# A hybrid decoder layer: stride-16 attention units multiply q with their own 128 key columns instead of 256

## The chip, the cores and the metric

The kernel runs on one core of one Trainium2 chip, as one launch. The metric is the time of an execution on the device in microseconds (us). TensorE (PE) multiplies into PSUM, VectorE (DVE) and ScalarE (ACT) read PSUM and work in SBUF, GpSimd (POOL) and SyncE (SP) issue most of the transfers. All data are 4 bytes wide: plain float32, or float32r, a rounded float32 which PE takes as a type of its own.

## The reference

One layer of a decoder with four parallel branches (pooling, dilated attention, short convolution, sliding-window attention) over a prompt of 2048 rows, and one decode step for 8 samples. What matters here is the dilated attention of the prompt: 6 heads of 64, each attended three times, at strides 1, 4 and 16, and mixed by the softmax of the three log-denominators. A stride d folds the 2048 rows into d residues of 2048/d rows; in each, row i reads the rows i-128 to i.

```python
DIL_CONFIGS = ((128, 1), (512, 4), (2048, 16))
def _fold(a, d):
    n, l, h, dh = a.shape
    return a.reshape(n, l // d, d, h, dh).transpose(0, 2, 1, 3, 4).reshape(n * d, l // d, h, dh)
def _dilated_prompt(q, k, v, slopes):
    for window, d in DIL_CONFIGS:
        o, lse = _band_attention(_fold(q, d)[:, :, :, None], _fold(k, d), _fold(v, d), slopes[:, None], d)
...
    return _mix_dilations(outs, lses)
```

In `_band_attention`, for each block of 128 rows with the 128 rows before it:

```python
    s = jnp.einsum("nbqhgd,nbkhd->nbhgqk", qb, kw, preferred_element_type=jnp.float32) * (1.0 / math.sqrt(dh))
    s = jnp.where(valid[None, :, None, None], s + bias, -jnp.inf)
    p = jnp.exp(s - m[..., None])
    o = jnp.einsum("nbhgqk,nbkhd->nbqhgd", p.astype(v.dtype), vw, preferred_element_type=jnp.float32)
```

At stride 16 a residue has exactly 128 rows, so it is one block with no block before it: its 128 queries need 128 keys, masked to the causal half.

## The kernel before, in words

The program has three parts. First the input projection: 30 tiles of 128 output columns, each product of a high and a low half in three matmuls (lines 929 to 931). Then the attention of the prompt, in three rounds, of which each takes two dilated heads; between these, the decode step's pieces. Then the output projection, row block by row block, with the same lines 929 to 931.

A round is a list of units; a unit is one block of 128 queries for two heads. Rounds one and two have 64 units: 16 at stride 1, 16 at stride 4, 16 at stride 16, and 16 of the sliding window (also stride 1). Round three has 48 and takes them in the order stride 16, 4, 1. The class `Unit` (line 455) gives for a unit its residue `r`, its block `b`, and the slices of q, keys and values. q, and the keys as a high and a low half (`kh_st`, `kl_st`), lie in SBUF as 128 partitions by 2048 rows in float32r, so that a residue at stride 16 is every 16th column: 128 columns, 64 bytes apart.

On PE the body of a round (`attend`, line 1109) runs in steps; step s issues the scores of unit s (line 1022), the transposes of unit s-3's probabilities (line 1038, matmuls at line 1045), the value product of unit s-5 (line 1048, matmuls at line 1061), and every fourth step the transposes of four outputs (line 1070). The scores are two matmuls a head, q times the high and q times the low half of the keys (lines 1034 and 1035), q being the operand that is loaded as weights and the keys the one that streams. They go to one of two PSUM banks, 256 columns a head; before a bank is used again PE waits for VectorE's pass over it (`x_ready`).

VectorE adds the bias and takes the minimum (line 1694), ScalarE takes the exponential (line 1302), PE transposes the probabilities, VectorE copies them out of PSUM (lines 1680 and 1682), PE multiplies them with the values. A unit that has a block before it (`full`) takes all 256 columns through this, any other 128: `own` says at which column these begin, `cols` and `halves` use it.

At stride 16 no unit is full. Its scores nevertheless stream 256 keys: `keys` returns the columns of two neighbouring residues, and `own` is 0 for the even one of them and 128 for the odd one, so that VectorE, ScalarE and the transposes take the right half, and the other half of PSUM is left unread.

VectorE also works on the decode step inside the rounds (lines 1578 to 1592 in rounds one and two, `decode` in round three). The loads of the next pair's q, keys and values are issued by SyncE when the last stride-16 unit's values are done (lines 725 to 727), since they overwrite the tiles that the units read.

Of the kernel before, what the change touches and what calls it, by code (L numbers as in the profile page):

```python
# [19 lines left out]
P = 128  # L20
# [55 lines left out]
def build_program(nc, x_prompt, x_sample, c_t, w_ada, b_ada, norm_g, w_tiles, const, pool_w, pool_scale,  # L76
# [4 lines left out]
    with ExitStack() as ctx:  # L81
# [4 lines left out]
        class Plan:  # L86

            def __init__(self, at):
                self.at = at
# [161 lines left out]
        psum = ctx.enter_context(nc.psum_tensor("psum", [P, 8, 512], F32))  # L251
# [203 lines left out]
        class Unit:  # L455

            def __init__(self, kind, c, i):
                self.kind, self.c, self.i = kind, c, i
                d = 1 if kind else DILATIONS[c]
                self.r, self.b = (0, i) if d == 1 else (i // 4, i % 4) if d == 4 else (i, 0)  # L460
                self.d = d
                self.full = self.b > 0

                self.own = P if self.full or (d == 16 and self.r % 2) else 0

            def view(self, t):
                return t[:].rearrange("p (t r) -> p r t", r=self.d)
# [4 lines left out]
            def keys(self, stack, h):  # L472
                v = self.view(stack[self.kind][h])
                if self.d == 16:
                    r0 = self.r - self.r % 2
                    return v[:, r0:r0 + 2, :]
                c0 = P * (self.b - 1) if self.full else 0
                return v[:, self.r, c0:c0 + 256]

# [30 lines left out]
        S_BANK, PT_BANK, OT_BANK, ON_BANK, DEC_BANK = 0, 2, 4, 6, 7  # L510
# [371 lines left out]
        def _(pe):  # L882
# [139 lines left out]
            def scores(base, n, u, i):  # L1022
                if u.kind and u.i == 0:
                    pe.wait_ge(swa_loaded, 16 * SWA_DMAS * (i + 1))
                if n == 0 and u.c:
                    for j in range(4):
                        pe.wait_ge(piece_loaded[j], 16 * PIECE_DMAS * (i + 1))
                if not u.kind and u.c == 0 and u.i % 4 == 0:
                    pe.wait_ge(piece_loaded[u.i // 4], 16 * PIECE_DMAS * (i + 1))
                if n >= 2:  # L1030
                    pe.wait_ge(x_ready, base + n - 1)
                for h in range(2):
                    out = psum[:, S_BANK + n % 2, 256 * h:256 * h + 256]
                    pe.matmul(out, u.q(h), u.keys(kh_st, h), start=True, stop=False)  # L1034
                    m = pe.matmul(out, u.q(h), u.keys(kl_st, h), start=False, stop=True)  # L1035
                m.then_inc(s_done, 1)
# [72 lines left out]
            def attend(i, us):  # L1109
                base, gbase, n = 64 * i, 16 * i, len(us)  # L1110
                for s in range(n + OUT_LAG + 1 - 4):
                    if len(us) < len(units):
                        decode(s)
                    if s < n:
                        scores(base, s, us[s], i)
                    if TURN_LAG <= s < n + TURN_LAG:
                        turn_probs(base, s - TURN_LAG, us[s - TURN_LAG])
                    if PV_LAG <= s < n + PV_LAG:
                        weigh_values(i, base, gbase, s - PV_LAG, us[s - PV_LAG])
                    if s >= OUT_LAG and (s - OUT_LAG) % 4 == 0:  # L1120
                        turn_out(gbase, (s - OUT_LAG) // 4)
# [825 lines left out]
```

## Time and profile before

| | us |
|---|---|
| median of 3 runs | 1496.07 (1495.25 to 1500.08) |
| span of the profiled execution, first to last instruction | 1494.0 |
| PE busy | 1370.9 (92%) |
| VectorE busy | 715.1 (48%) |
| ScalarE busy | 462.9 (31%) |
| score matmuls, lines 1034 and 1035, 352 each | 148.9 and 123.9 |
| transposes of probabilities, line 1045 | 96.8 |
| value products, line 1061 | 102.5 |

The page lists no time of the profiled execution beside its span; the runs' median lies 2.07 us above that span. Busy times of PE overlap one another, since a matmul's record runs to its last write, so the distance between starts tells more than a duration. PEld are the weight loads, which run beside the matmul before. The attention lies between 828 and 1233 us of the span: round one to 964, round two from 971 to 1103, round three from 1114. The granted clock is given in parts of 2.4 GHz; it has two levels, 1.2 and 2.4 GHz, so that 0.50 in a stretch means that all of it ran at 1.2.

### The profile page before, as it was taken

What the parts mean: (1) busy time and instruction counts of PE and PEld (TensorE: products, weight loads), DVE (VectorE), ACT (ScalarE), POOL (GpSimd) and SP (SyncE); (2) the same over time, 40 slices, a digit from 0 to 9 for tenths busy, and PEclk for the clock granted to TensorE, in tenths of its full rate; (3) what the DMA queues carried; (4) which work ended last, traced back from release to release, by engine and by line L of the source; (5) the groups of instructions that cost most, each with busy time, mean ns of one, the idle gap of its engine ahead of it and who ended that gap; (6) DMA issues with size and microseconds to landing.
All of it is one profiled execution on the core that took longest, in us unless ns stands there. A gap on an engine that the chain in (4) does not pass through costs nothing.

```text
span 1494.0 us, 21742 instructions
## 1 busy us (share of the span) xinstructions
PE 1370.9 (92%) x7749; PEld 1189.5 (80%) x7749; DVE 715.1 (48%) x1835; ACT 462.9 (31%) x1190; POOL 155.0 (10%) x170
## 2 busy tenths in 40 slices
PE   5779999999999999999996799799969997999996
PEld 2376999999999998999996687588757765877774
DVE  3491111100344544132112557676767646788784
ACT  5530000121111001121111455565647641433331
POOL 0060000000122110000000012101110000111111
PEclk9989999999999999999998799999989998999998
DMA  8613121221353434446435992972394255555531
GB/s 311 220 55 121 57 84 42 84 84 43 113 198 121 149 114 141 128 118 167 104 80 127 250 264 85 240 202 63 92 267 132 87 173 177 158 174 155 174 126 45
DMA packets 127167, 206.34 MB, mean 138 GB/s; under 512 B 14339, under 2 KB 89764, under 8 KB 121549
## 3 DMA queue, kind: packets, MB, share of 16 engines
q1 hardware_dynamic: 113862, 160.13, 36.7%
q0 software_dynamic: 13216, 45.09, 9.1%
q8 instruction: 48, 0.79, 0.2%
q14 instruction: 41, 0.34, 0.1%
HBM read 136.34 MB, written 68.97 MB: 137 GB/s over the span
## 4 chain that ended last, share of the span: by engine, by line
PE 68%; issue 14%; DVE 6%; DMA 4%; SPq 4%; ACT 2%; POOL 2%; DVEq 0%; POOLq 0%; ACTq 0%
PE psum L929 15%; PE psum L930 14%; PE psum L931 14%; PE psum L1034 5%; PE psum L1061 5%; PE psum L1045 4%; PE psum L1035 4%; SPq L427 2%; PE psum L900 2%; DMA dil_v_p<-kv_nat 2%; PE psum L1070 1%; POOL resid L876 1%; DVE h_f L1435 1%; DMA v_dil<-dil_v_p 1%; PE psum L1103 1%
## 5 line engine op out<-in xcount | busy, mean ns | idle before, releaser
L929 PE MATMUL psum<-h_hi,w_hi 128*128 128x416 f32 (+1 forms) x1200 | 422.9, 352 | 12.7 <-POOL h_lo L808 12.6
L930 PE MATMUL psum<-h_lo,w_hi 128*128 128x416 f32 (+1 forms) x1200 | 420.8, 351 | 0.0
L931 PE MATMUL psum<-h_hi,w_lo 128*128 128x416 f32 (+1 forms) x1200 | 419.5, 350 | 0.0
L929 PEld LDWEIGHTS psum<-h_hi,w_hi 128*128 128x128 f32 x1200 | 226.7, 189 | 17.7 <-issue 14.9
L930 PEld LDWEIGHTS psum<-h_lo,w_hi 128*128 128x128 f32 x1200 | 226.6, 189 | 1.5
L931 PEld LDWEIGHTS psum<-h_hi,w_lo 128*128 128x128 f32 x1200 | 226.4, 189 | 1.3
L1302 ACT ACTIVATE probs<-logits,stats 128x256 f32<-128x256 f32 (+1 forms) x352 | 162.2, 462 | 172.2 <-DVE stats L1694 169.7
L1034 PE MATMUL psum<-kh_st,q_st 128*128 128x256 f32 x352 | 148.9, 431 | 40.4 <-DMA v_dil<-dil_v_p 30.6
L1694 DVE CUSTOM_DVE_ANT_0 logits<-psum,bias_dil 128x256 f32<-128x256 f32 (+1 forms) x288 | 94.4, 363 | 108.0 <-PE psum L1035 88.5
L1034 PEld LDWEIGHTS psum<-kh_st,q_st 128*128 128x128 f32 x352 | 93.5, 266 | 63.7 <-issue 38.0
L929 PE MATMUL psum<-wo_hi,y_hi 128*128 128x512 f32 x288 | 116.8, 406 | 11.0 <-DVE y_lo L1764 10.6
L1035 PE MATMUL psum<-kl_st,q_st 128*128 128x256 f32 x352 | 123.9, 361 | 0.0
L931 PE MATMUL psum<-wo_hi,y_lo 128*128 128x512 f32 x288 | 113.9, 396 | 0.0
L930 PE MATMUL psum<-wo_lo,y_hi 128*128 128x512 f32 x288 | 113.8, 395 | 0.0
L1515 DVE SCALAR_TENSOR_TENSOR main_lo<-psum,main_hi 128x416 fp32r<-128x416 f32 (+1 forms) x45 | 26.2, 583 | 164.8 <-ACT main_hi L1264 164.8
L1508 DVE COPY main<-psum 128x416 f32<-128x416 f32 (+1 forms) x60 | 34.2, 582 | 143.6 <-PE psum L931 143.6
L1045 PE MATMUL psum<-consts,probs 128*128 128x128 f32 x574 | 96.8, 283 | 3.4 <-DVE probs_t L1682 3.4
L1216 ACT CAST w_hi<-w_raw 128x1024 fp32r<-128x1024 f32 x30 | 31.3, 1043 | 211.3 <-PE psum L931 189.2
L1035 PEld LDWEIGHTS psum<-kl_st,q_st 128*128 128x128 f32 x352 | 96.0, 273 | 0.0
L1680 DVE COPY probs_t<-psum 128x512 f32<-128x512 f32 x111 | 76.7, 691 | 23.5 <-PE psum L1061 22.8
L1061 PE MATMUL psum<-probs_t,v_dil 128*64 128x128 f32 x900 | 82.1, 291 | 0.0
L1045 PEld LDWEIGHTS psum<-consts,probs 128*128 128x128 f32 x574 | 73.0, 146 | 9.3 <-issue 6.8
(244 smaller groups left out, 1560.2 us busy)
## 6 DMA issues: line engine op xcount, KB each, us to landing
w_raw<-w_tiles POOLq DMA_DIRECT2D x30, 512.0 KB, 5.9
mix_dram<-o_st POOLq DMA_DIRECT2D x36, 264.0 KB, 3.6
mix_in<-mix_dram SPq DMA_DIRECT2D x16, 594.0 KB, 4.0
gate_dram<-main SPq DMA_DIRECT2D x9, 1024.0 KB, 3.9
qk_dram<-main_hi SPq DMA_DIRECT2D x18, 512.0 KB, 6.1
qk_dram<-main_lo SPq DMA_DIRECT2D x18, 512.0 KB, 7.8
x_in<-x_prompt SPq DMA_DIRECT2D x16, 512.0 KB, 5.9
ada_w<-w_ada SPq DMA_DIRECT2D x4, 2048.0 KB, 10.0
```

The source lines that it names most:

```text
L929: pe.matmul(out, hi, mhi, start=start, stop=False)
L930: pe.matmul(out, hi, mlo, start=False, stop=False)
L931: return pe.matmul(out, lo, mhi, start=False, stop=stop)
L1034: pe.matmul(out, u.q(h), u.keys(kh_st, h), start=True, stop=False)
L1035: m = pe.matmul(out, u.q(h), u.keys(kl_st, h), start=False, stop=True)
L1045: m = pe.transpose(psum[:, PT_BANK + n % 2, P * k:P * k + P], probs[n % 4][:, h, c:c + P], ident)
L1061: m = pe.matmul(psum[64 * h:64 * h + 64, OT_BANK + g % 2, P * (n % 4):P * (n % 4) + P], u.v(h, back), probs_t[n % 2][:, k, :], start=(x == ...
L1216: nc.scalar.copy(w_hi[b][:], w_raw[b][:]).then_inc(w_hi_ready, 1)
L1302: m = nc.scalar.activation(probs[s % 4][:, h, u.cols()], xs_[s % 2][:, h, u.cols()], ACT.Exp, scale=-1.0, bias=st[:, s % 4, 2 * h:2 * h + ...
L1508: last = dve.tensor_copy(main[b][:, c0:c0 + n], bank(g, n))
L1680: dve.tensor_copy(dst[:], src).then_inc(pt_copied, 1)
L1694: m = dve.tensor_tensor_reduce(out=xs_[s % 2][:, h, c], in0=psum[:, S_BANK + s % 2, 256 * h + c.start:256 * h + c.stop], in1=u.bias(h), sc ...
```

## The change

A unit at stride 16 streams its own residue's 128 keys: `keys` returns one residue, the matmul's output is 128 columns wide instead of 256, and `own` is 0 for odd residues too, so that these use PSUM columns 0 to 127 of their head's 256 like the even ones. Units at strides 1 and 4 and of the window stay as they are. The number and the order of the instructions on every engine are the same before and after; in the listing of PE's instructions 128 rows differ (those of a loop's body and of round three), each by its number of columns, 128 instead of 256. In an execution these are 192 matmuls.

```diff
@@ class Unit
-                self.own = P if self.full or (d == 16 and self.r % 2) else 0
+                self.own = P if self.full else 0
...
             def keys(self, stack, h):
                 v = self.view(stack[self.kind][h])
                 if self.d == 16:
-                    r0 = self.r - self.r % 2
-                    return v[:, r0:r0 + 2, :]
+                    return v[:, self.r, :]
...
@@ scores, on PE
                 for h in range(2):
-                    out = psum[:, S_BANK + n % 2, 256 * h:256 * h + 256]
+                    out = psum[:, S_BANK + n % 2, 256 * h:256 * h + (P if u.d == 16 else 256)]
                     pe.matmul(out, u.q(h), u.keys(kh_st, h), start=True, stop=False)
                     m = pe.matmul(out, u.q(h), u.keys(kl_st, h), start=False, stop=True)
```

## Rows read from the trace of the kernel before

**Rows 1.** Page, head and part 1: engine, busy us (share) xinstructions.

```profile
span 1494.0 us, 21742 instructions
...
PE 1370.9 (92%) x7749; PEld 1189.5 (80%) x7749; DVE 715.1 (48%) x1835; ACT 462.9 (31%) x1190; POOL 155.0 (10%) x170
```

**Rows 2.** Page, part 4: chain of waits by line, share of span.

```profile
PE psum L929 15%; PE psum L930 14%; PE psum L931 14%; PE psum L1034 5%; PE psum L1061 5%; PE psum L1045 4%; PE psum L1035 4%; SPq L427 2%; PE psum L900 2%; DMA dil_v_p<-kv_nat 2%; PE psum L1070 1%; POOL resid L876 1%; DVE h_f L1435 1%; DMA v_dil<-dil_v_p 1%; PE psum L1103 1%
```

**Rows 3.** Stretches: us, busy us (count): PE PEld DVE ACT POOL; clock, DMA, GB/s.

```profile
914.00:926.00 12.00, 12.00 (x72) 9.78 (x72) 7.25 (x28) 6.80 (x28) 4.79 (x8) 1.00 0.45 121
...
1130.00:1140.00 10.00, 10.00 (x60) 8.04 (x60) 7.35 (x31) 8.62 (x29) 0.39 (x1) 1.00 0.24 61
```

**Rows 4.** Timeline, stride-16 unit: start us, us, engine, line, operation.

```profile
913.75 0.29 PEld L1034 LDWEIGHTS psum<-kh_st,q_st 128*128 128x128 f32 x1 [0.17 <-issue]
...
913.96 0.31 PEld L1035 LDWEIGHTS psum<-kl_st,q_st 128*128 128x128 f32 x1
...
914.39 0.31 PEld L1035 LDWEIGHTS psum<-kl_st,q_st 128*128 128x128 f32 x1
...
914.59 0.40 PE L1035 MATMUL psum<-kl_st,q_st 128*128 128x256 f32 x1
...
914.64 0.32 PEld L1045 LDWEIGHTS psum<-consts,probs 128*128 128x128 f32 x2
...
914.80 0.40 PE L1045 MATMUL psum<-consts,probs 128*128 128x128 f32 x2
...
915.50 0.29 PEld L1034 LDWEIGHTS psum<-kh_st,q_st 128*128 128x128 f32 x1 [0.17 <-issue]
```

**Rows 5.** Timeline, PE and PEld, end of a window unit's scores (stride 1).

```profile
944.50 0.19 PEld L1035 LDWEIGHTS psum<-kl_st,q_st 128*128 128x128 f32 x1
944.61 0.29 PE L1035 MATMUL psum<-kl_st,q_st 128*128 128x256 f32 x1
944.63 0.47 PEld L1045 LDWEIGHTS psum<-consts,probs 128*128 128x128 f32 x4
944.74 0.60 PE L1045 MATMUL psum<-consts,probs 128*128 128x128 f32 x4
```

**Rows 6.** Timeline, PEld, first weight load of the third round.

```profile
1114.10 0.29 PEld L1034 LDWEIGHTS psum<-kh_st,q_st 128*128 128x128 f32 x1 [10.90 <-issue]
```

**Rows 7.** Groups by line and shape: busy us, mean ns of one.

```profile
L1034 PE MATMUL psum<-kh_st,q_st 128*128 128x256 f32 x352 | 148.9, 431 | 40.4 <-DMA v_dil<-dil_v_p 30.6 <-issue 7.1 <-DVE stats L1694 2.7
...
L1061 PEld LDWEIGHTS psum<-probs_t,v_dil 128*64 128x64 f32 x900 | 47.1, 137 | 24.8 <-issue 20.8 <-DVE probs_t L1680 3.5 <-DVE probs_t L1682 0.5
```

**Rows 8.** Waits of PE: us in total, times, longest us.

```profile
PE psum L1045 <- DVE probs_t L1682: 3.4, 8, 0.7
PE psum L1034 <- DVE stats L1694: 2.7, 3, 1.9
```

**Rows 9.** Timeline, PE, two neighbouring stride-16 units, third round.

```profile
1123.70 0.56 PE L1034 MATMUL psum<-kh_st,q_st 128*128 128x256 f32 x1
...
1125.88 0.60 PE L1034 MATMUL psum<-kh_st,q_st 128*128 128x256 f32 x1
```

**Rows 10.** Timeline, SP's queue, then PE: the second pair's load.

```profile
936.65 0.32 SPq L420 DMA_DIRECT2D q_st<-qk_dram  x1
...
970.81 0.57 PE L1034 MATMUL psum<-kh_st,q_st 128*128 128x256 f32 x1 [7.12 <-issue]
```

**Rows 11.** Chain in order of time: a decode product on PE.

```profile
1187.31 1.92 PE psum L1103 x6
```

**Rows 12.** Stretches, columns as above: three parts of the program.

```profile
32.00:35.00 3.00, 1.70 (x14) 1.22 (x12) 1.90 (x3) 2.97 (x5) 0.00 (x0) 1.00 0.69 233
...
1070.00:1074.00 4.00, 2.22 (x14) 1.51 (x14) 3.82 (x10) 1.43 (x5) 0.00 (x0) 0.86 0.22 68
1122.00:1126.00 4.00, 4.00 (x20) 3.08 (x18) 2.03 (x14) 2.87 (x14) 0.00 (x0) 0.50 0.81 262
```

## The prediction, made before the changed kernel ran

> **What bounds the kernel now.** Read first the head of the page: TensorE (PE) is busy 1370.9 of 1494.0 us [rows 1]; then the chain of waits, where the projection's three lines hold 43% and the two score lines L1034 and L1035 only 9% [rows 2]. The change touches these two score lines alone, and there only the units at stride 16, so the next view is the table of stretches over the stride-16 units: there PE is busy all the time at the granted clock 1.00, the 2.4 GHz level (12.00 of 12.00 us), VectorE 7.25 and ScalarE 6.80 [rows 3]. PE sets the pace there, so what matters is what paces PE, and that is read from the timeline of one unit.
>
> A stride-16 unit lasts from its first weight load at 913.75 to the next unit's at 915.50, 1.75 us. Its four score matmuls each bring their own load of 128 q columns. The loads start at 913.75, 913.96 and, the fourth, at 914.39: one every 0.215 us. The fourth matmul starts at 914.59, the load for the transposes at 914.64, the first transpose at 914.80 [rows 4]. In a unit of the sliding window, whose q and keys lie side by side, the fourth load starts only 0.11 us before its matmul, and the matmul 0.13 us before the first transpose [rows 5].
>
> Is 0.215 us the price of the load or of the 256 keys? Two things take that long at stride 16. A load alone on an engine that had been idle for 10.90 us takes 0.29 us [rows 6] against 0.19 for the window's [rows 5]. Loads of 64 adjacent columns average 137 ns [rows 7], so 64 columns cost 52 ns more, 128 cost 0.105, and a fixed 0.085 remains; taken from 0.29 to 0.31 us that leaves 0.21 to 0.22 for reading 128 q columns at stride 16. So the load by itself explains the 0.215 us. The fourth matmul is followed by the first transpose after 0.21 us although that transpose's load began 0.16 us before it, where the window needed 0.11: so the 256 strided keys also take about 0.21 us, and hide exactly behind the next load.
>
> The Trainium skill ("TensorE: Matmul & The Clock Gate", section "LDWEIGHTS (loading the stationary operand)") has a load cost its columns over 1.2 GHz, 107 ns for 128, with no word on stride. By that and its "Back-to-back issue gap" section (262 cycles for 256 columns at 2.4 GHz, 134 for 128) load and matmul cost about 108 ns each now and the load stays; the estimated gain would be the last matmul's 53 ns in a unit, 1.5 us over the 29 units counted below. The window's rows agree with the 107 ns, the stride-16 rows are twice that; the conclusion that the load remains is the same.
>
> **The change part by part.** (1) 192 matmuls (3 rounds x 16 units x 2 heads x hi and lo) read 128 keys instead of 256. No instruction is removed, added or moved on any engine, and the 192 weight loads stay as they are. With the loads every 0.215 us, the first three matmuls of a unit gain nothing by being shorter; only the fourth has no strided load behind it. Halved, it ends about 0.105 us earlier, but the transposes' load starts at 914.64 and needs 0.11 us as in the window, so the first transpose moves from 914.80 to 914.75: 0.05 us. If that load also starts 0.02 us after the matmul as in the window, not 0.05, it is 0.08. I take **0.06 us a unit**; the ends are 0 (the load holds the transposes where they are) and 0.105 (the whole half matmul).
>
> (2) Not every unit passes this on. In rounds one and two VectorE has three pieces of decode work among the stride-16 units, and PE then waits for the copied probabilities (8 such waits, 3.4 us, of which the timeline has one a round in the window's units) [rows 8]; each wait swallows the gain of some two units, so 10 of 16 remain. In round three the first seven units wait for a load, for VectorE (up to 1.9 us [rows 8]) and run partly at the low clock; 9 remain. That makes 29 units: 29 x 0.06 = **1.7 us**. Nothing takes it back later: the load of the second pair's keys is issued when the stride-16 values are done (936.65), and PE waits for it until 970.81 [rows 10], so that chain moves as a whole.
>
> (3) Odd units write PSUM and probability columns 0 to 127 instead of 128 to 255. VectorE, ScalarE and the transposes handle the same 128 columns; I cost it at nothing, and their spare time covers a few ns: VectorE is busy 0.60 and ScalarE 0.57 of the first round's stretch, 0.74 and 0.86 of the third's [rows 3].
>
> The sum is -1.7 us on a span of 1494.0; the median of the runs, 1496.07, lies 2.07 above that span, which I carry along: 1496.07 - 1.7 = 1494.4. A measurement of this kernel tells about 0.3% (4.5 us) from no change, so this is no change. The bounds are 0 and 48 x 0.105 = 5.0 us.
>
> **The rivals.** *Keys, not loads, set the 0.215 us (faster).* Were the 0.29 us load only slow in its record, each of the four matmuls would fall to the window's 0.11 us: 0.4 us a unit. Rounds one and two gain 20 x 0.4 = 8; in round three ScalarE's 0.86 of 1.75 us, 1.51, is the next bound, 9 x 0.24 = 2. Together 10, giving 1486. Against it stands the slow load on an idle engine [rows 6]; for it, that matmul and load take the same time, so that no row of a unit separates them.
>
> *Narrow matmuls in this type are dearer per column (no change).* All matmuls on fp32r operands in the trace have 256 columns or more, so the price of 128 is not shown. The nearest row for a dearer one is plain fp32: three decode products of 384 columns take 1.92 us [rows 11], 1.67 ns a column, 0.213 us for 128. That is what 256 strided keys take now, so at the high clock nothing changes; in the six or so units at the low clock, where it would double, up to 0.85 us each is partly covered by the waits of round three. 1496 to 1499, I say 1497.
>
> *The same, with a second weight load (slower).* Plain fp32 matmuls leave two records and two loads each (900 loads for 450 value products, against 352 records for 352 score matmuls [rows 7]). If narrow score matmuls did so too, each would cost another 0.215 us: 48 x 0.86 = 41, less some 5 in waits, 1532. It decides as soon as the count of L1034's records is above 352.
>
> *The clock falls (slower).* With half the keys, PE does less between loads. The granted clock was 0.86 around 1070 to 1074, where PE was busy 2.22 of 4.00 us, and 0.50 at 1122 to 1126 though PE was busy throughout; against that, 1.00 at 32 to 35 with 1.70 of 3.00 us of transposes alone [rows 12]. A stride-16 unit at the 1.2 GHz level takes 1125.88 - 1123.70 = 2.18 us [rows 9] instead of 1.75, so 0.43 more. Over the 29 units that PE paces it is 12.5 less the 1.7: 1507. It decides when more than some 10 of the units run low (4.3 us).
>
> **How the numbers follow.** My forecast has 0.58, dearer narrow matmuls 0.15, keys setting the pace 0.11, a second load 0.06, a falling clock 0.10. The first two are within 0.3%, except for 0.01 of the first at its far end: faster 0.12, same 0.72, slower 0.16. The likeliest time is 1494.4. For 8 in 10 the range takes the first two cases (1491 to 1499) and reaches into the third and the last: 1488 to 1504.
>
> **What would show it.** Right: L1034 and L1035 still have 352 records each, 96 of them with 128 columns; the loads of these still take 0.30 us and one every 0.21 us; the first transpose 0.16 us behind the fourth matmul instead of 0.21; the unit at 1.69 us; clock 1.00 in the stride-16 stretches. Loads closer than 0.2 us prove the first rival, a clock of 0.5 there the last; matmul starts more than 0.22 us apart at the high clock, or more records, mean that a narrow matmul is dear. I am wrong if the unit moves by more than 0.15 us either way.

## The result: slower by 0.7%, and the profile after

The changed kernel takes **1503.84 us** (median of 5 runs, 1503.24 to 1512.19), the kernel before beside it 1495.44 (5 runs, 1493.96 to 1500.08). The ratio is 1.007, with a 95% interval of 1.0045 to 1.0095: the loss is well above the 0.3% below which a measurement of this kernel counts as no change. The profiled execution has a span of 1500.8 us; the span before was 1494.0 [rows 1].

In the changed kernel the lines behind the edit are numbered one lower: the scores are L1033 and L1034, the transposes L1044, the value products L1060. The head of its page, its last line the granted clock of TensorE (PE) in 40 slices of 37.5 us, in tenths of full speed:

```profile
span 1500.8 us, 21742 instructions
...
PE 1378.8 (92%) x7749; PEld 1191.4 (79%) x7749; DVE 716.5 (48%) x1835; ACT 462.7 (31%) x1190; POOL 155.0 (10%) x170
...
PEclk9989999999999999999997998899775997999999
```

The counts are those of before, and PE, which was to work less, is busy 7.9 us longer. The reason stands in the last line: the 25th slice (900 to 938 us) has an 8, the 29th (1051 to 1088) a 7 and the 31st (1126 to 1163) a 5. Each holds part of one round's units at stride 16. In the kernel before all three slices have a 9:

```profile
PEclk9989999999999999999998799999989998999998
```

Cut exactly from the first score record of the first stride-16 unit to the first of the unit behind the sixteenth, the three stretches of the kernel before read as follows (us; busy us and count of PE, weight loads PEld, VectorE, ScalarE, POOL; granted clock, DMA share, GB/s):

```profile
894.59:927.29 32.70, 31.71 (x200) 25.24 (x198) 22.79 (x87) 17.54 (x73) 7.89 (x13) 1.00 0.34 98
1033.15:1065.85 32.70, 31.71 (x200) 25.24 (x199) 22.74 (x87) 17.54 (x73) 7.90 (x13) 1.00 0.29 84
1114.13:1144.72 30.59, 27.93 (x149) 22.13 (x149) 20.98 (x90) 18.63 (x70) 0.75 (x1) 0.84 0.50 141
```

And of the changed kernel, with one more line for six microseconds inside its first stretch and one that answers to [rows 3]:

```profile
890.05:924.58 34.53, 33.50 (x200) 25.89 (x198) 22.98 (x87) 17.46 (x73) 7.90 (x13) 0.80 0.33 96
1030.76:1065.87 35.11, 34.05 (x201) 26.06 (x199) 23.54 (x91) 18.41 (x77) 7.91 (x13) 0.77 0.29 83
1115.20:1150.05 34.85, 32.20 (x148) 23.56 (x148) 22.18 (x92) 18.92 (x71) 0.75 (x1) 0.50 0.42 123
908.00:914.00 6.00, 6.00 (x31) 4.03 (x30) 2.55 (x15) 3.34 (x14) 2.41 (x4) 0.50 0.43 113
...
1130.00:1140.00 10.00, 10.00 (x50) 7.00 (x49) 5.55 (x25) 6.35 (x21) 0.00 (x0) 0.50 0.19 54
```

The rounds lose 1.83, 2.41 and 4.26 us, together 8.5; the medians differ by 8.4. (The profiled span differs by 6.8: in that execution the attention also began 4.15 us earlier, at 824.07 instead of 828.22, and all the rest took 2.5 longer.) The granted clock fell from 1.00 to 0.80 and 0.77 in the first two rounds, and in the third from 0.84 to 0.50, the 1.2 GHz level throughout. In the last two lines PE has no idle time in its records and is still at 1.2 GHz; from 1130 to 1140 it gets through 50 matmul records where it had 60.

A unit of the changed kernel, at either clock. First at 2.4 GHz, its timeline of weight loads and then of PE (start us, us, engine, line, operation):

```profile
918.52 0.30 PEld L1033 LDWEIGHTS psum<-kh_st,q_st 128*128 128x128 f32 x1 [0.17 <-issue]
918.73 0.31 PEld L1034 LDWEIGHTS psum<-kl_st,q_st 128*128 128x128 f32 x1
918.94 0.31 PEld L1033 LDWEIGHTS psum<-kh_st,q_st 128*128 128x128 f32 x1
919.16 0.31 PEld L1034 LDWEIGHTS psum<-kl_st,q_st 128*128 128x128 f32 x1
919.41 0.22 PEld L1044 LDWEIGHTS psum<-consts,probs 128*128 128x128 f32 x2
...
919.25 0.40 PE L1034 MATMUL psum<-kl_st,q_st 128*128 128x128 f32 x1
919.47 0.40 PE L1044 MATMUL psum<-consts,probs 128*128 128x128 f32 x2
919.80 0.44 PE L1060 MATMUL psum<-probs_t,v_dil 128*64 128x128 f32 x4
920.17 0.47 PE L1033 MATMUL psum<-kh_st,q_st 128*128 128x128 f32 x1
```

From 918.52 to 920.17 it takes 1.65 us, 0.10 less than before [rows 4]. The loads still start 0.21 us apart and still take 0.30 us; what came forward is the transposes. Then at 1.2 GHz, PE alone:

```profile
909.70 0.49 PE L1033 MATMUL psum<-kh_st,q_st 128*128 128x128 f32 x1
910.00 0.41 PE L1034 MATMUL psum<-kl_st,q_st 128*128 128x128 f32 x1
910.22 0.41 PE L1033 MATMUL psum<-kh_st,q_st 128*128 128x128 f32 x1
910.44 0.41 PE L1034 MATMUL psum<-kl_st,q_st 128*128 128x128 f32 x1
910.66 0.64 PE L1044 MATMUL psum<-consts,probs 128*128 128x128 f32 x2
911.22 0.70 PE L1060 MATMUL psum<-probs_t,v_dil 128*64 128x128 f32 x4
911.85 0.49 PE L1033 MATMUL psum<-kh_st,q_st 128*128 128x128 f32 x1
```

From 909.70 to 911.85 it is 2.15 us. From the second on, the score matmuls start 0.22 us apart as at the high clock; the half us is lost in the transposes (0.56 us to the next line's start, against 0.33) and the value products (0.63 against 0.37).

### The profile page after: what moved, and what is told of

Its sections match the earlier page's. It is cut to its first block, busy times and chain, and to the rows that moved or that the text cites. A ratio compares the mean times of both kernels' runs of the same rounds, so it can differ in the third digit from the quotient of the medians.

```text
span 1500.8 us, 21742 instructions
## 1 busy us (share of the span) xinstructions
PE 1378.8 (92%) x7749; PEld 1191.4 (79%) x7749; DVE 716.5 (48%) x1835; ACT 462.7 (31%) x1190; POOL 155.0 (10%) x170
## 4 chain that ended last, share of the span: by engine, by line
PE 69%; issue 14%; DVE 5%; SPq 4%; DMA 3%; ACT 2%; POOL 2%; DVEq 0%; POOLq 0%; ACTq 0%
PE psum L928 15%; PE psum L929 15%; PE psum L930 15%; PE psum L1060 5%; PE psum L1033 5%; PE psum L1044 4%; PE psum L1034 4%; SPq L427 2%; PE psum L899 2%; PE psum L1069 2%; POOL resid L875 1%; DVE h_f L1434 1%; DMA v_dil<-dil_v_p 1%; PE psum L1102 1%; DMA ada_w<-w_ada 1%
## 5 line engine op out<-in xcount | busy, mean ns | idle before, releaser
L1033 PE MATMUL psum<-kh_st,q_st 128*128 128x256 f32 (+1 forms) x352 | 143.9, 418 | 44.0 <-DMA v_dil<-dil_v_p 33.7
L1033 PEld LDWEIGHTS psum<-kh_st,q_st 128*128 128x128 f32 x352 | 93.3, 265 | 69.5 <-issue 36.7
L928 PE MATMUL psum<-wo_hi,y_hi 128*128 128x512 f32 x288 | 117.3, 407 | 10.8 <-DVE y_lo L1763 10.5
L1034 PE MATMUL psum<-kl_st,q_st 128*128 128x256 f32 (+1 forms) x352 | 124.2, 361 | 0.0
L1044 PE MATMUL psum<-consts,probs 128*128 128x128 f32 x574 | 102.0, 293 | 3.4 <-DVE probs_t L1681 3.4
L1034 PEld LDWEIGHTS psum<-kl_st,q_st 128*128 128x128 f32 x352 | 95.7, 272 | 0.0
L1060 PE MATMUL psum<-probs_t,v_dil 128*64 128x128 f32 x900 | 88.1, 306 | 0.0
L1044 PEld LDWEIGHTS psum<-consts,probs 128*128 128x128 f32 x574 | 71.3, 150 | 7.5 <-issue 5.9
```

The source lines that it names most:

```text
L928: pe.matmul(out, hi, mhi, start=start, stop=False)
L1044: m = pe.transpose(psum[:, PT_BANK + n % 2, P * k:P * k + P], probs[n % 4][:, h, c:c + P], ident)
L1060: m = pe.matmul(psum[64 * h:64 * h + 64, OT_BANK + g % 2, P * (n % 4):P * (n % 4) + P], u.v(h, back), probs_t[n % 2][:, k, :], start=(x == ...
```

## The experiments

Seven more kernels ran, each beside runs of the kernel before on the same chip (median 1492.56 us of 29 runs for e1 to e4, 1492.6 of 25 for e5 to e7). The table has the three stretches, cut as above, of every profiled execution: length in us, and granted clock in brackets. "Narrow" are the score matmuls at stride 16 that read 128 keys.

| kernel | narrow per unit | round 1 | round 2 | round 3 | ratio to before |
|---|---|---|---|---|---|
| before | none | 32.70 (1.00) | 32.70 (1.00) | 30.59 (0.84) | |
| the change | all 4 | 34.53 (0.80) | 35.11 (0.77) | 34.85 (0.50) | 1.007 |
| e1 | none, other columns | 32.71 (1.00) | 32.73 (1.00) | 30.77 (0.83) | 0.9997 |
| e2 | all 4, and one more matmul | 33.63 (1.00) | 33.66 (1.00) | 34.83 (0.50) | one run |
| e3 | 1st and 2nd | 32.74 (1.00) | 32.73 (1.00) | 33.30 (0.62) | 1.0033 |
| e4 | 4th | 31.67 (1.00) | 31.65 (1.00) | 29.34 (0.78) | 0.9976 |
| e5 | 2nd and 4th | 31.66 (1.00) | 31.91 (0.95) | 32.21 (0.62) | 0.9989 |
| e6 | all 4, rounds 1 and 2 | 36.13 (0.69) | 31.87 (0.95) | 30.40 (0.80) | 1.0043 |
| e7 | all 4, round 3 | 32.74 (1.00) | 32.73 (1.00) | 34.79 (0.50) | 1.0025 |

Single executions of one kernel differ by several us (those of e4 by 10), and a profile shows one of them; so a stretch is read by its own length and clock, and the ratio from all runs. The mean granted clock of the whole execution is on record for every run and agrees: 0.964 to 0.970 in the 54 runs of the kernel before, 0.965 to 0.970 in e1, 0.961 to 0.971 in e4, 0.960 to 0.970 in e5, 0.958 to 0.965 in e3, 0.957 to 0.964 in e7, 0.949 to 0.958 in e6 and 0.941 to 0.949 in the five of the change.

**e1, the columns alone.** The matmuls stay wide; the two residues that an odd unit streams are now its own and the next, so that odd units use PSUM columns 0 to 127 as in the change. Residue 15 has no next one; it still comes second, behind residue 14.

```diff
-                self.own = P if self.full or (d == 16 and self.r % 2) else 0
+                self.own = P if self.full or (d == 16 and self.r == 15) else 0
...
-                    r0 = self.r - self.r % 2
+                    r0 = min(self.r, 14)
```

> All stride-16 score matmuls stream 256 keys again, but with the unit's own residue first (its pair is the residue behind it), so that all units but those of residue 15 use PSUM columns 0 to 127. Theory (the granted clock falls because the narrow matmuls give PE less to do): the three stride-16 stretches last as before, 32.7, 32.7 and 30.6 us, the first two at clock 1.00, and the time is that of the kernel before, within 0.2%. Rival (the changed PSUM columns of the odd units cost the time): the stretches last 34.5, 35.1 and 34.9 us and the time is 0.5% above that of the kernel before.

Measured: 1492.37 us (10 runs, 1488.62 to 1495.61), ratio 0.9997 (0.9983 to 1.0011), stretches as before. The other columns cost nothing; the loss comes from the narrow matmuls.

**e2, narrow with other work put back.** The change, and in rounds 1 and 2 one more matmul of 512 columns after each stride-16 unit's scores.

```diff
+                if u.d == 16 and not isinstance(i, int):
+                    pe.matmul(psum[:, DEC_BANK, :], kh_st[0][0][:, 0:P], kh_st[0][0][:, 0:512], start=True, stop=True)
```

> The changed kernel, with one more matmul behind the scores of each stride-16 unit in rounds one and two: 512 adjacent columns into a PSUM bank that nothing reads then. Theory (clock): in these two rounds the clock stays at 1.00 and no unit takes the 2.15 us of the low clock; a unit free of waits takes 1.65 plus some 0.22 us for the added matmul, so each stretch lasts 34 to 36 us in spite of 16 more matmuls. Round three, without the addition, stays at clock 0.50 and 34.9 us. Rival (narrow matmuls are dearer by themselves, whatever the clock): the units keep their 2.15 us and get the addition on top, 37 us and more for each of the two stretches.

Measured: 1502.77 us in one run. Its three stretches:

```profile
892.06:925.69 33.63, 33.60 (x216) 26.84 (x215) 22.99 (x87) 17.47 (x73) 7.89 (x13) 1.00 0.34 98
1032.91:1066.57 33.66, 33.62 (x217) 26.87 (x215) 23.00 (x87) 17.47 (x73) 7.91 (x13) 1.00 0.29 83
1116.13:1150.96 34.83, 32.21 (x148) 23.54 (x148) 22.18 (x92) 18.91 (x71) 0.75 (x1) 0.50 0.41 122
```

With 16 more matmuls in each of the first two, these stretches are 0.9 and 1.45 us shorter than the change's 34.53 and 35.11, and the clock is 1.00; the third, where nothing was added, is the change's to 0.02 us and stays at 0.50. So a narrow matmul is not dear in itself. The stretches are also shorter than the 34 to 36 us expected: PE's waits inside them are gone (busy 33.60 of 33.63 us, where it was 31.71 of 32.70 before), which the expectation had not counted. The added work stands on the path:

```profile
918.46 0.39 PE L1034 MATMUL psum<-kl_st,q_st 128*128 128x128 f32 x1
918.67 0.43 PE L1036 MATMUL psum<-kh_st 128*128 128x512 f32 x1
918.94 0.38 PE L1046 MATMUL psum<-consts,probs 128*128 128x128 f32 x2
```

0.27 us a unit, from 918.67 to 918.94: the clock stays up with it, but it costs more than the 0.10 that the narrow unit saves, so padding is no way to win here.

**e3, head 0 narrow.** The score line takes this form in e3, with `keys` giving the own residue where narrow and e1's two residues where wide; e4 to e7 differ from it in the line `wide` alone, which is what their diffs show:

```diff
-                    out = psum[:, S_BANK + n % 2, 256 * h:256 * h + 256]
-                    pe.matmul(out, u.q(h), u.keys(kh_st, h), start=True, stop=False)
-                    m = pe.matmul(out, u.q(h), u.keys(kl_st, h), start=False, stop=True)
+                    for part, st in ((0, kh_st), (1, kl_st)):
+                        wide = u.d < 16 or h == 1
+                        c = 256 * h + (0 if wide else u.own)
+                        m = pe.matmul(psum[:, S_BANK + n % 2, c:c + (256 if wide else P)], u.q(h), u.keys(st, h, wide),
+                                      start=(part == 0), stop=(part == 1))
```

> Only head 0's two score matmuls of a stride-16 unit stream 128 keys, head 1's stream 256: three quarters of the columns. Theory (clock, and one narrow matmul is enough to let the matmuls catch up with the weight loads): every unit at the high clock still takes 0.10 us less than before; the clock stays up in rounds one and two, which then last 31.3 us each, or falls in part; time 1491 to 1499. Rival (each narrow matmul adds a cost of its own): half of the change's loss, 1499 to 1500, with the clock at 1.00.

Measured: 1497.95 us (10 runs, 1492.06 to 1504.01), ratio 1.0033 (1.0016 to 1.005): slower. In rounds 1 and 2 the clock held, and nothing was saved. PE's timeline of a unit there, its first two matmuls narrow:

```profile
916.18 0.47 PE L1038 MATMUL psum<-kh_st,q_st 128*128 128x128 f32 x1
916.47 0.39 PE L1038 MATMUL psum<-kl_st,q_st 128*128 128x128 f32 x1
916.69 0.50 PE L1038 MATMUL psum<-kh_st,q_st 128*128 128x256 f32 x1
917.01 0.40 PE L1038 MATMUL psum<-kl_st,q_st 128*128 128x256 f32 x1
917.24 0.40 PE L1049 MATMUL psum<-consts,probs 128*128 128x128 f32 x2
...
917.93 0.47 PE L1038 MATMUL psum<-kh_st,q_st 128*128 128x128 f32 x1
```

The fourth matmul, wide, is followed by the transposes after 0.23 us and the unit takes 1.75 us, as before. A shorter matmul ahead of the last gives nothing, as the prediction had it; my expectation that any narrow matmul in a unit would do was the miss. In round 3 the clock is 0.62 and the stretch is 2.7 us longer, for no gain. (The three stretches of this one execution lose 2.8 us, 0.19%, inside the interval of the ratio.)

**e4, only the last matmul narrow.**

```diff
-                        wide = u.d < 16 or h == 1
+                        wide = u.d < 16 or (h, part) != (1, 1)
```

> Only the last of the four score matmuls of a stride-16 unit (head 1, low half of the keys) streams 128 keys: 7 of 8 parts of the columns. Theory (clock; the fourth narrow matmul alone lets the transposes start when their load is there): clock 1.00 in the stretches of rounds one and two, 31.3 us each against 32.7, and some 1.2 us less in round three: 4 us less than the kernel before, 0.25%. Rival (the narrow matmul saves nothing by itself): the time of the kernel before.

Measured: 1487.71 us (12 runs, 1485.01 to 1494.96), ratio **0.9976** (0.996 to 0.9993): faster than both kernels. Its stretches, then the end of a unit, weight loads and PE:

```profile
888.33:920.00 31.67, 30.09 (x200) 24.16 (x199) 22.81 (x87) 17.48 (x73) 7.92 (x13) 1.00 0.37 110
1027.02:1058.67 31.65, 30.10 (x200) 24.14 (x199) 22.74 (x87) 17.48 (x73) 7.93 (x13) 1.00 0.29 83
1105.36:1134.70 29.34, 26.70 (x149) 21.18 (x149) 20.98 (x90) 18.68 (x70) 0.75 (x1) 0.78 0.48 137
```

```profile
906.97 0.58 PE L1038 MATMUL psum<-kh_st,q_st 128*128 128x256 f32 x1
...
907.80 0.29 PE L1038 MATMUL psum<-kl_st,q_st 128*128 128x128 f32 x1
907.91 0.40 PE L1049 MATMUL psum<-consts,probs 128*128 128x128 f32 x2
...
908.61 0.57 PE L1038 MATMUL psum<-kh_st,q_st 128*128 128x256 f32 x1
...
907.86 0.21 PEld L1049 LDWEIGHTS psum<-consts,probs 128*128 128x128 f32 x2
```

The narrow matmul is followed by the transposes after 0.11 us (907.80 to 907.91) instead of 0.21 [rows 4], the unit takes 1.64 us, and the stretches lose 1.03, 1.05 and 1.25 us, together 3.3 us (0.22%, beside the 0.24% of the ratio). The clock is 1.00 in two rounds and 0.78 in the third. So a quarter of the edit has all of its gain, and almost none of its cost.

**e5, the low halves of both heads narrow** (2nd and 4th matmul).

```diff
-                        wide = u.d < 16 or h == 1
+                        wide = u.d < 16 or part == 0
```

> The low half of the keys streams 128 columns for both heads, the high half 256: three quarters of the columns as with a narrow head 0, but here the last matmul of a unit is a narrow one. Theory (the saving is that of the last matmul, 0.10 us a unit; the clock goes by how much the four stream together): rounds one and two at clock 1.00 and 31.7 us each, as with the last matmul alone; round three with a lower clock than before's 0.84 and 31 to 33 us; time between the kernel before and 4 us below it. Rival (any second narrow matmul in a unit takes the saving back): units of 1.75 us, 32.7 us a round.

Measured: 1491.52 us (10 runs, 1486.94 to 1500.77), ratio 0.9989 (0.9967 to 1.0011), no change. The first round is e4's (31.66); the second ran at 0.95, the third at 0.62 and is 1.6 us longer than before. The 4th matmul brings the gain, the 2nd adds nothing to it and costs clock.

**e6, all four narrow in rounds 1 and 2, and e7, in round 3 alone.**

```diff
-                        wide = u.d < 16 or h == 1
+                        wide = u.d < 16 or isinstance(i, int)
...
-                        wide = u.d < 16 or h == 1
+                        wide = u.d < 16 or not isinstance(i, int)
```

> All four score matmuls narrow in rounds one and two, none in round three. Theory (clock, each round by itself): 34 to 35.5 us for the stretches of rounds one and two at clock 0.75 to 0.85, 30.6 us for round three at 0.84; 3 to 5 us above the kernel before. Rival (the low clock of round three is handed on from the earlier rounds): round three near 34.9 us here too.

> All four score matmuls narrow in round three alone. Theory (clock): 32.7 us at clock 1.00 in rounds one and two, 34.9 us at 0.50 in round three: 4 us above the kernel before. With the rounds-one-and-two variant this adds up to the whole change's loss. Rival (handed on): round three near 30 us, and the time that of the kernel before.

Measured: e6 1497.53 us (10 runs, 1495.16 to 1507.72), ratio 1.0043 (1.0021 to 1.0065); e7 1496.62 us (10 runs, 1493.55 to 1502.44), ratio 1.0025 (1.0006 to 1.0045). Together 0.43 + 0.25 = 0.68%, the change's 0.70% well within the intervals: the first two rounds lose without narrow matmuls in the third, and the third loses without them in the first two. In e7's profile the first two rounds are as before and the third as in the change (34.79, 0.50). In e6's profile two rounds that run the same loop body differ:

```profile
889.46:925.59 36.13, 35.65 (x200) 26.87 (x198) 23.66 (x91) 18.43 (x77) 7.92 (x13) 0.69 0.32 92
1033.06:1064.93 31.87, 30.85 (x200) 24.66 (x199) 22.82 (x87) 17.47 (x73) 7.92 (x13) 0.95 0.30 80
```

The first ran mostly at 1.2 GHz and lost 3.4 us; the second had 0.95 and gained 0.8. That is a miss for the expectation, which had both alike, and it shows that the loss goes with the clock and not with the code: same instructions, 4.3 us apart.

## Why the prediction was wrong

**What failed is the step that left the granted clock where it was.** The sum of -1.7 us has no term for the clock, 1.00 in the stride-16 stretches was a sign of being right, and a falling clock stood among the rivals with a chance of 0.10, where the forecast of no change had 0.58. Measured were 0.80, 0.77 and 0.50, and a unit at the low clock takes 2.15 us, 0.40 more than before, where 0.15 was to be the sign of being wrong.

That rival was right in that the clock falls and in what this costs a unit. Its reason, that PE does less between loads, was not separated from others (below). Its size was near, 10.8 us worked out against 8.4 measured, and in part by luck, since two of its terms were off in opposite ways. It had 0.43 us for a unit at the low clock, measured 2.15 - 1.65 = 0.50 between narrow units; and it had 29 units, measured as (8.5 + 3.3) / 0.50, some 24 (the 3.3 is what narrow units give where the clock holds, from e4). These are 6 and 7 in the first two rounds and 11 in the third, since the rest of that round waits anyway or was already slow before. The measured 1503.84 us lies just inside the range of 1488 to 1504, which reached so far for this rival; the forecast itself, no change, did not come true.

**The row that misled** was the stretch of transposes at 32 to 35 us, 1.70 of 3.00 us busy with a clock of 1.00 [rows 12]. I took it as showing that little work on PE holds the clock. The row beside it, 1122 to 1126 at 0.50 with PE busy 4.00 of 4.00, came from the very units that the change makes lighter, and it shows that a busy PE can be at the low clock; I let the far row outweigh the near one. The third round begins at 1.2 GHz in both kernels, after PE's wait for a load, and the four microseconds behind that row tell them apart. The kernel before, then the changed one, columns as in [rows 3]:

```profile
1126.00:1130.00 4.00, 4.00 (x21) 3.14 (x22) 2.04 (x11) 1.57 (x9) 0.00 (x0) 0.81 0.00 0
...
1126.00:1130.00 4.00, 4.00 (x20) 2.95 (x20) 1.77 (x10) 1.90 (x10) 0.00 (x0) 0.50 0.16 64
```

PE is equally busy in both. With wide matmuls the clock comes back here; with narrow ones it is at 0.50 to the end of the stretch at 1150.05.

**Part (1), what a unit gains, was right in its mechanism and too small.** The loads pace the first three matmuls (loads still 0.21 us apart in the change; no gain in e3), and the fourth alone gains (e4). The term was 0.06 us a unit, measured 0.10 to 0.11, the upper end: I had the transposes' load need 0.11 us before the first transpose, as in the window [rows 5]; in e4 the transpose starts 0.05 us behind it (907.86, 907.91), so the whole half of the matmul is saved. In the change itself, from the fourth load to the transposes it is 0.31 us (919.16 to 919.47), where it was 0.41 [rows 4]. The sign given for it, transposes 0.16 us behind the fourth matmul, did not show, since that matmul now starts sooner behind its load: they follow after 0.22.

**Part (2)**, 29 units that pass it on: e4's 3.3 us over 0.11 is 30. The waits that swallow the rest are there: in the first stretch of e4 PE waits 0.48, 0.47 and 0.56 us for the copied probabilities, in that of the kernel before 0.23, 0.41 and 0.35. **Part (3)**, the columns at nothing: e1 shows it. With the right size the sum at an unchanged clock would have been 29 x 0.11 = 3.2 us, which is e4's time, not the change's.

**The other rivals.** Keys do not set the 0.21 us: it stayed with half the keys. Nor is there a second load: the groups of the changed kernel hold 256 wide and 96 narrow records on either line, with 352 loads:

```profile
L1034 PE MATMUL psum<-kl_st,q_st 128*128 128x256 f32 x256 | 85.5, 346 | 0.0
L1034 PE MATMUL psum<-kl_st,q_st 128*128 128x128 f32 x96 | 38.7, 403 | 0.0
L1034 PEld LDWEIGHTS psum<-kl_st,q_st 128*128 128x128 f32 x352 | 95.7, 272 | 0.0
```

A narrow matmul is not dear either: in e4 it takes 0.11 us, half of the wide one's 0.21. (The mean of 403 ns above 346 is no price: records overlap, and the narrow matmuls of the change start 0.22 us apart.)

**What stays open.** That the clock goes with the number of narrow matmuls in a unit is shown by the third round: 0.80 to 0.84 with none (three kernels), 0.78 with one, 0.62 with two (e3, e5), 0.50 with four (the change, e2, e7); one cannot be told from none. Which property of them does it was not separated: they stream fewer columns, and they also leave PE waiting within a unit for the next load (0.11 us in e4 against starts 0.21 us apart), which the records do not show.

Nor do narrow matmuls alone decide it. In the change's first stretch the clock stayed at 1.00 through six narrow units, and fell after PE had waited 0.48 us for VectorE's copied probabilities:

```profile
901.83 0.41 PE L1044 MATMUL psum<-consts,probs 128*128 128x128 f32 x2 [0.48 <-DVE probs_t L1681]
...
902.00:904.00 2.00, 2.00 (x12) 1.37 (x10) 2.00 (x8) 1.87 (x9) 0.00 (x0) 0.82 0.41 125
```

All five falls in the stretches of the first two rounds (two in the change, two in e6, one in e5) came after such a wait, of 0.48 to 0.52 us. The wait alone is not enough, since e4 has as long ones at 1.00:

```profile
900.11 0.41 PE L1049 MATMUL psum<-consts,probs 128*128 128x128 f32 x2 [0.48 <-DVE probs_t L1686]
```

In e2's two padded stretches these waits are gone, so it is not shown whether the added matmul kept the clock by its columns or by closing them. And the clock also came back with narrow units running: to 1.00 by 918 in the change, and within the second stretch of e6. What decides between 0.69 and 0.95 for the same code in e6 is not settled.

The Trainium skill ("TensorE: Matmul & The Clock Gate", section "A second HAM failure mode: psum-queue depth-cycling") tells of a kernel whose clock swings because PE is idle for moments between groups of matmuls, not on waits for a DMA. PE's records from 908 to 914 cover 6.00 of 6.00 us, so no idle moment is to be seen there, and e4 had the waits of half a microsecond without a fall; no run here shows that this is the cause.

## What to carry to other kernels

Where a change makes TensorE's work lighter but not shorter, because something else paces it, price the granted clock too. Read the clock of the nearest stretches of the same kind, and don't take PE's busy share for it: here they stood at 1.00 [rows 3] and at 0.50 [rows 12], with PE busy throughout in both, and that was a warning. Where weight loads pace a chain of matmuls, as in these units, only the last matmul's width is on the path; make that one narrow and leave the others wide (e4: 0.24% faster, against 0.7% slower for all four).

## What the runs showed of the hardware

- TensorE can be at 1.2 GHz with no idle time in its records: 6.00 of 6.00 us in round 1, 10.00 of 10.00 in round 3. With one more matmul of 512 columns in each unit, 0.27 us, it was at 2.4 GHz in both rounds where this was tried (e2, one run).
- In these stretches of the first two rounds the clock fell only in kernels with two or four narrow matmuls a unit, and each time after PE had waited 0.48 to 0.52 us (five falls); with one narrow matmul, waits as long left it at 1.00 (e4).
- The weight loads of 128 columns at stride 16 start 0.21 to 0.22 us apart at either clock level, with 128 keys or 256; between the two units of the change shown above, the low clock costs time in the transposes and the value products alone (0.23 and 0.26 us).
- By the records, a transpose can start 0.05 us after its weight load begins (e4), not only after the 0.11 of the window's rows.
